# Third feed-forward: two products of 256 tokens a pass in its first stage, two row halves of the array in its last

## The reference, cut to what matters

```python
h2 = rms_norm(x, g_norm2[l]) * (1.0 + sc2) + sh2
f = jnp.square(jax.nn.relu(h2 @ w_ff1[l])) @ w_ff2[l]      # (512,1024) @ (1024,4096), then @ (4096,1024)
x = x + gt2 * f
```

## Time and profile before

| what | us |
|---|---|
| three runs | 3152.48, 3153.67, 3173.94 |
| their median | 3153.67 |
| profiled execution, span from first to last instruction | 3159.8 |
| PE busy | 3075.4 (97%) |
| PE weight loads busy | 2387.5 (76%) |
| DVE, ACT, POOL busy | 1608.0, 1172.9, 1269.7 |

### The profile page before, as it was taken

How to read it: one execution, slowest core, us unless ns; L and a number is a source line. 1 busy time by engine, 2 the same in 40 slices (tenths; PEclk the granted TensorE clock), 3 DMA queues, 4 the chain that set the end, 5 groups by cost and what they waited for, 6 DMA issues and landing times.

```text
span 3159.8 us, 58989 instructions
## 1 busy us (share of the span) xinstructions
PE 3075.4 (97%) x23906; PEld 2387.5 (76%) x23906; DVE 1608.0 (51%) x2435; ACT 1172.9 (37%) x1615; POOL 1269.7 (40%) x655
## 2 busy tenths in 40 slices
PE   7999999999999999999999999899999999899999
PEld 5758888868688886888887877678888674458887
DVE  6655555067465555566564641664141786644140
ACT  5413444223354443444334323443232433532231
POOL 3333444434143331444454434344444364224443
PEclk9999999999999999999999999999999999999999
DMA  4212333323100001444563322023333222023333
GB/s 138 80 54 70 97 94 99 107 73 98 50 3 3 3 3 43 145 140 151 186 201 110 96 78 87 27 94 94 100 94 99 67 67 68 8 86 95 100 94 100
DMA packets 74612, 268.63 MB, mean 85 GB/s; under 512 B 8719, under 2 KB 8730, under 8 KB 74240
## 3 DMA queue, kind: packets, MB, share of 16 engines
q1 hardware_dynamic: 73536, 262.53, 26.6%
q0 software_dynamic: 896, 3.52, 0.4%
HBM read 261.71 MB, written 2.10 MB: 83 GB/s over the span
## 4 chain that ended last, share of the span: by engine, by line
PE 88%; issue 5%; DVE 3%; ACT 2%; POOL 1%; DMA 1%; SPq 0%; DVEq 0%; POOLq 0%; ACTq 0%
PE gp L383 66%; PE gp L1304 5%; PE aux L1304 1%; PE gp L2524 1%; PE gp L3187 1%; PE aux L1299 1%; PE gp L1324 1%; PE gp L847 1%; POOL w_low L358 1%; PE aux L1441 1%; DMA ring<-in_weights 1%; PE gp L1374 1%; PE aux L3131 1%; PE aux L1404 1%; PE aux L3210 0%
## 5 line engine op out<-in xcount | busy, mean ns | idle before, releaser
L358 POOL TENSOR_TENSOR w_low<-ring,w_high 128x1024 fp32r<-128x1024 f32 x413 | 1002.0, 2428 | 1456.3 <-ACT w_high L328 1455.8
L328 ACT ACTIVATE w_high<-ring 128x1024 fp32r<-128x1024 f32 x413 | 437.0, 1059 | 974.3 <-DMA ring<-in_weights 972.0
L383 PE MATMUL gp<-ffn_h,w_high 128*128 128x512 f32 x2432 | 750.6, 390 | 2.7 <-POOL w_low L358 1.1
L383 PEld LDWEIGHTS gp<-ffn_h,w_high 128*128 128x128 f32 x2432 | 455.9, 188 | 101.8 <-issue 3.7
L383 PE MATMUL gp<-ffn_h,w_low 128*128 128x512 f32 x1216 | 473.2, 389 | 0.0
L383 PE MATMUL gp<-ffn_high,w_high 128*128 128x512 f32 x928 | 361.0, 389 | 0.0
L383 PE MATMUL gp<-ffn_low,w_high 128*128 128x512 f32 x864 | 336.1, 389 | 0.0
L383 PE MATMUL gp<-ffn_high,w_low 128*128 128x512 f32 x864 | 336.1, 389 | 0.0
L383 PE MATMUL gp<-in_h,w_high 128*128 128x512 f32 x896 | 279.5, 393 | 0.0
L383 PEld LDWEIGHTS gp<-ffn_h,w_low 128*128 128x128 f32 x1216 | 228.2, 188 | 47.4
L2424 DVE TENSOR_TENSOR arena<-arena 128x512 f32<-128x512 f32 x64 | 100.3, 1568 | 217.8 <-ACTq L163 215.1
(11 more groups left out here) (575 smaller groups left out, 5058.6 us busy)
## 6 DMA issues: line engine op xcount, KB each, us to landing
ring<-in_weights SPq DMA_DIRECT2D x437, 512.0 KB, 3.6
H<-in_ada SPq DMA_DIRECT2D x48, 512.0 KB, 4.4
arena<-arena SPq DMA_DIRECT2D x32, 67.5 KB, 2.0
X<-in_x SPq DMA_DIRECT2D x4, 512.0 KB, 7.4
out_x<-X SPq DMA_DIRECT2D x8, 256.0 KB, 4.4
arena<-in_sm POOLq DMA_DIRECT2D x1, 1024.0 KB, 4.9
cst<-in_cst SPq DMA_DIRECT2D x1, 756.0 KB, 9.7
arena<-in_hy_f_w POOLq DMA_DIRECT2D x1, 512.0 KB, 5.5
```

The costliest lines, as they stand in the source:

```text
L328: nc.scalar.activation(w_high[:, slab % RING, :], ring[:, slab % RING, :], ACT.Copy).then_inc(high_ready, 1)
L358: nc.gpsimd.tensor_tensor(w_low[:, slab % RING, :], ring[:, slab % RING, :], w_high[:, slab % RING, :], ALU.subtract).then_inc(low_ready, 1)
L383: last = nc.tensor.matmul(gp[:, t.bank, :], wt[:, slab % RING, w], x(k), start=(k == 0 and q == 0), stop=(k == sum(kt) - 1 and q == 2))
```

## The change

In `ff1a_3` each pass becomes two products of 256 tokens, each with its own load of the same weights, into the two column halves of the same bank; only the first of a tile's products has `start` set, which concerns the whole bank. In `ff2b_3` each pass becomes two products over 64 input channels each: partitions 0 to 63 of weights and activations go into the bank of `gp`, partitions 64 to 127 into the bank of `aux` with the same number. DVE then adds both banks to `X`, one after the other, before it reports the tile. `ff1b_3`, `ff2a_3` and all other feed-forwards stay as they are.

```diff
-        def split_pe(pe, name, high, low, ksizes=None, before=None, body=8, beside=None, between=None, opening=0):
+        def split_pe(pe, name, high, low, ksizes=None, before=None, body=8, beside=None, between=None, opening=0, halves=False,
+                     rows=False):
...
-                    last = nc.tensor.matmul(gp[:, t.bank, :], wt[:, slab % RING, w], x(k), start=(k == 0 and q == 0),
-                                            stop=(k == sum(kt) - 1 and q == 2))
+                    first, final = k == 0 and q == 0, k == sum(kt) - 1 and q == 2
+                    if rows:
+                        for bank, r in ((gp, slice(0, 64)), (aux, slice(64, P))):
+                            last = nc.tensor.matmul(bank[:, t.bank, :], wt[r, slab % RING, w], x(k)[r], start=first, stop=final)
+                    elif halves:
+                        for c in (slice(0, S // 2), slice(S // 2, S)):
+                            last = nc.tensor.matmul(gp[:, t.bank, c], wt[:, slab % RING, w], x(k)[:, c],
+                                                    start=(first and c.start == 0), stop=final, skip_group_check=True)
+                    else:
+                        last = nc.tensor.matmul(gp[:, t.bank, :], wt[:, slab % RING, w], x(k), start=first, stop=final)
...
-                             opening=AHEAD, beside=beside)
+                             opening=AHEAD, beside=beside, halves=b == 3)
...
-                         before=lambda k: pe.wait_ge(f_ready, first + k + 1))
+                         before=lambda k: pe.wait_ge(f_ready, first + k + 1), rows=b == 3 and i == 1)
...
-        def gated_residual_dve(dve, v, name, gate, body=8, sq=None):
+        def gated_residual_dve(dve, v, name, gate, body=8, sq=None, rows=False):
...
+                if rows:
+                    v.settle()
+                    v.go(nc.vector.scalar_tensor_tensor(out=x, in0=aux[:, t.bank, :], scalar=MOD(gate, t.idx), in1=x,
+                                                        op0=ALU.mult, op1=ALU.add))
...
-                gated_residual_dve(dve, v, f"ff2{'ab'[i]}_3", 5)
+                gated_residual_dve(dve, v, f"ff2{'ab'[i]}_3", 5, rows=i == 1)
```

## The result

| | median us | runs |
|---|---|---|
| before, with the runs made beside the changed kernel | 3157.64 | 18 (3152.48 to 3173.94) |
| after | 3163.06 | 18 (3158.41 to 3174.28) |

The ratio is 1.0022, with a 95% interval of 1.0012 to 1.0031: slower by 3.8 to 9.8 us, a change that 18 runs can tell from none and that is far inside 1%. The profiled execution of the changed kernel took 3168.79 us, with a span of 3166.8.

The account below looks back on a forecast made before the run. The prediction took PE's pace of a pass as the bound. Its terms, +3.5 - 0.3 + 0 + 0.9 = +4.1 us on the median of 3153.7, gave 3158 us, no change that can be told, range 3148 to 3180 us, chance 0.80.

Parts of the forecast that it names:

- PE's pace bounds the four stages: In the third feed-forward's four stages PE is busy almost throughout, so the pace of a pass, 0.227 us, decides.
- First edit, +3.5 us: In `ff1a_3`, splitting 384 passes into two 256-column products each was to cost 9 ns a pass, +3.5 us.
- upper bound of +5.0: Highest cost allowed for the `ff1a_3` split: 13 ns more on each of 384 passes, +5.0 us.
- The direct pair in the earlier trace: Two 256-column products in the profile before: the second adds 0.12 us, so 0.24 us a pass, 13 ns more.
- The difference of means in the earlier trace: Mean pair lengths by width: 256 columns fewer save 111 ns, so 116 ns a product, 5 ns more a pass.
- The POOL wait: PE's 0.7 us wait for POOL's `w_low` in `ff1a_3` was to shrink through slower passes: -0.3 us.
- The load is not the bound: In `ff1a_3` loads can follow every 0.11 us, under the product's 0.116 to 0.12; rival at 188 ns: 3212 us, chance 0.05.
- Second edit, 0 us: In `ff2b_3` two row-half products run side by side and cost one whole product, as in f32: 0 us.
- The doubt about the rate of writing: In `ff2b_3` fp32r halves must write two banks twice as fast as any row shows; rival taking turns: 3245 us, chance 0.09.
- half overlap: Rival in `ff2b_3`: the second half starts one load later and the next pair waits, 0.34 us a pair, 3200 us, chance 0.05.
- The end, +0.9 us: After `ff2b_3`'s last tile, DVE's second addition takes 0.75 us plus at most 0.18 for settling: +0.9 us.
- The sum: Over the changed stages, +3.5 - 0.3 + 0 + 0.9 = +4.1 us, giving 3158 us.

Follow-up runs that it names:

- the uneven products: Changed kernel with `ff1a_3` in products of 320 and 192 columns a pass and `ff1b_3` in 384 and 128: 0.260 and 0.287 us a pass.
- the four-product stage: Changed kernel with each `ff2b_3` pass as four products, each row half for each half of the columns: the stage took 92 us.
- groups of three: Changed kernel with `ff2b_3` reordered: for each channel block, three products of rows 0 to 63, then three of rows 64 to 127; stage 87.0 us.
- groups of 24: Changed kernel with `ff2b_3` reordered: for each slab, 24 products of rows 0 to 63, then 24 of rows 64 to 127; stage 151 us.

## Why the prediction was right

- *PE's pace bounds the four stages.* Shown: the changed stage's length is its number of products times their pace, 768 x 0.120 = 92.2 us, plus 0.5 for start and waits; nothing else took it over.
- *First edit, +3.5 us.* Right in kind, under-sized: +13.3 ns a pass instead of 9, 384 x 13.3 = +5.1 us, just over its own upper bound of +5.0. I had split the difference between two readings. The direct pair in the earlier trace rows (0.12 us for the second product) held. The difference of means in the earlier trace rows, 111 ns, did not: it compares lengths of rows, while the starts in the trains lie 226.7 and 120.0 ns apart, which is 106.7 less. The mixture of first and second products in these means is not the reason, since the second products alone (392 to 395 and 282 to 284 ns) differ by 111 as well. The POOL wait gave back 0.5 us instead of 0.3.
- *The load is not the bound.* Shown by the uneven products: 0.113 us a load, against 0.120 for the product. The recorded 0.19 us is a load's length, not its pace. The reading from the earlier trace rows came out at the right number partly by luck, as the f32 columns alone take as long. And the rule that the prediction takes from the Trainium skill's page "TensorE: Matmul & The Clock Gate", section "Part 3: Packing small matmuls — row/col tiling", that a load hides only behind products of other row groups, does not hold in these traces: the loads of `ff1a_3` are under way for 92.3 of its 92.7 us, all of them beside products of the same rows.
- *Second edit, 0 us.* Shown: 87.3 us, products of both halves starting together in fp32r. The doubt about the rate of writing was unfounded, and half overlap did not occur; the four-product stage shows that the loads of the halves run side by side too.
- *The end, +0.9 us.* 0.8 measured: the second addition starts 0.03 us behind the end of the first, where the bound for settling was 0.18.
- *The sum.* +4.1 forecast, +5.6 in the changed stages, +3.8 to +9.8 by the runs. The median after, 3163 us, lies 5 above the forecast: 1.5 of it is the changed stages, of which 1.3 the mis-sized first edit, and the rest that the kernel before, over 18 runs, stood at 3157.6 and not at the 3153.7 of three. That the time stayed inside the forecast's 3148 to 3180 us needed no such precision; the stages show that the mechanism was right.

## What to carry to other kernels

A matmul train is priced from the distance between starts in a train or a pair, never from the length of a row: loads recorded at 0.19 us followed each other every 0.113. An fp32r product on the whole array cost 13.3 ns + 0.417 ns a column here, by the two widths of 512 and 256, with a floor of 0.113 us for its load. So splitting a pass of 512 columns in two costs 13 ns at 256 columns each, and more where one part has fewer than some 240, an estimate from where 13.3 + 0.417 n meets 113. Two row halves cost one whole product here if their products stood within three of each other in the program, and won nothing where the whole array was full already.

## What the runs showed of the hardware that was not expected

Products on different row halves overtook each other by up to three places: groups of three cost nothing (87.0 us), groups of 24 cost 64 us (151). A fixed part of 13.3 ns in each fp32r product shrinks to 7 with loads of 64 or 32 weight columns and 256 data columns, while whole passes of 512 columns rise from 0.227 to 0.230 us with the same narrow loads; no run explains it. In 236 us of unchanged code two traces differ by 41 products, some 9 us, which is more than either edit cost, and yet they reach the changed stages within 2.2 us of each other.
